# A block of conv, attention and experts: engine order from a list-scheduling pass

## The reference, cut to what matters

```python
mod = silu(c) @ w_ada + b_ada            # sh1, sc1, g1, sh2, sc2, g2, each 1024 wide
hc  = modulate(rmsnorm(ctx), csh1, csc1); k_ctx, v_ctx = context_kv(hc, w_in)
h   = modulate(rmsnorm(x), sh1, sc1)
b, cg, xin, q, k, v, ga, gb = split_in(h @ w_in)
ya  = (b * conv3(cg * xin)) @ w_a
yb  = window_attention(rope(q), rope(k), v, k_ctx, v_ctx, sink) @ w_b   # 8 heads, window 128
x   = x + g1 * ((sigmoid(ga) * ya + sigmoid(gb) * yb) @ w_o)
h   = modulate(rmsnorm(x), sh2, sc2)
x   = x + g2 * hierarchical_moe(h)       # 32 experts, top 2 of the best group
out = rmsnorm(x) * final_g
```

## Time and profile before

| | |
|---|---|
| median of 3 runs | 1257.78 us (1255.66 to 1257.82) |
| profiled execution | 1262.3 us; span of its slowest core, core 1, 1260.6 us |
| PE, DVE, ACT, POOL busy on core 1 | 852.7, 574.9, 394.2, 345.9 us |
| shortest span of a core | 1202.1 us (core 6) |
| DMA | 139.6 MB moved on core 1, mean 111 GB/s |

### The profile page before, as it was taken

The page is one execution under the profiler, slowest core; times in us unless marked ns, Lnnn a source line. Parts: engine busy times, 40 slices in busy tenths (PEclk is TensorE's granted clock), DMA queues, the critical chain, the costliest instruction groups (busy, mean ns, idle before and its releaser), DMA issues. The chain is left out here.

```text
span 1260.6 us, 15879 instructions; the slowest of 8 cores (1202.1 to 1260.6 us)
## 1 busy us (share of the span) xinstructions
PE 852.7 (68%) x6066; PEld 496.3 (39%) x6066; DVE 574.9 (46%) x956; ACT 394.2 (31%) x747; POOL 345.9 (27%) x346
## 2 busy tenths in 40 slices
PE   0035666688698998999999212688688888888500
PEld 0012323343344543444444111466466566666400
DVE  0016333336498133355555257544344344344498
ACT  0022222124344444533333121033233333334332
POOL 2000000022234122202020002356545555565200
PEclk9996878889789899999999755799899999989855
DMA  9952110059750301010206940169999798988473
GB/s 188 198 94 84 51 50 17 1 86 174 123 93 8 61 1 68 1 68 26 76 34 129 175 113 17 56 116 187 200 185 175 147 195 164 190 151 157 129 294 150
DMA packets 41228, 139.61 MB, mean 111 GB/s; under 512 B 14640, under 2 KB 19376, under 8 KB 33600
## 3 DMA queue, kind: packets, MB, share of 16 engines
q0 software_dynamic: 24544, 97.39, 42.3%
q1 hardware_dynamic: 16608, 41.21, 9.6%
HBM read 255.22 MB, written 37.22 MB: 232 GB/s over the span
## 5 line engine op out<-in xcount | busy, mean ns | idle before, releaser
L357 PE MATMUL ps<-sb 128*128 128x512 bf16 (+8 forms) x4976 | 792.6, 317 | 208.9 <-DVE sb L381 136.7
L357 PEld LDWEIGHTS ps<-sb 128*128 128x128 bf16 (+2 forms) x4976 | 428.9, 105 | 551.4 <-issue 182.3
L364 ACT ACTIVATE sb<-ps 128x512 bf16<-128x512 f32 (+4 forms) x593 | 317.3, 584 | 580.2 <-PE ps L357 474.8
L369 DVE TENSOR_TENSOR sb<-ps,sb 128x256 bf16<-128x256 f32 (+4 forms) x262 | 124.6, 482 | 339.7 <-PE ps L357 172.1
L378 DVE SCALAR_TENSOR_TENSOR sb<-sb 128x1024 f32<-128x1024 f32 (+6 forms) x125 | 140.8, 1136 | 12.7 <-DMA sb<-yd 10.0
L1054 POOL DMA_INDIRECT yd<-sb x94 | 99.6, 1059 | 146.0 <-ACT sb L364 132.5
L369 POOL TENSOR_TENSOR sb<-sb 128x1024 bf16<-128x1024 f32 x14 | 32.9, 2346 | 335.3 <-DVE sb L378 298.0
L669 POOL TENSOR_TENSOR sb<-sb 128x512 bf16<-128x512 bf16 x60 | 71.6, 1193 | 156.4 <-ACT sb L364 149.7
L1005 POOL DMA_INDIRECT sb<-hd,sb x94 | 96.7, 1028 | 61.6 <-DVE sb L896 33.6
L369 DVE TENSOR_TENSOR sb<-sb 128x512 bf16<-128x512 f32 (+4 forms) x113 | 86.8, 768 | 35.7 <-issue 31.1
L378 DVE SCALAR_TENSOR_TENSOR sb<-sb,ps 128x512 f32<-128x512 f32 x64 | 43.8, 687 | 129.0 <-PE ps L357 125.5
(11 more groups left out here) (37 smaller groups left out, 144.2 us busy)
## 6 DMA issues: line engine op xcount, KB each, us to landing
sb<-wex POOLq DMA_DIRECT2D x47, 1536.0 KB
sb<-x SPq DMA_DIRECT2D x32, 512.0 KB, 5.1
sb<-wad POOLq DMA_DIRECT2D x12, 1024.0 KB, 16.7
sb<-wsl POOLq DMA_DIRECT2D x8, 1024.0 KB, 44.1
sb<-yd SPq DMA_DIRECT2D x16, 512.0 KB, 5.7
out<-sb SPq DMA_DIRECT2D x16, 512.0 KB, 3.2
hd<-sb SPq DMA_DIRECT2D x16, 256.0 KB, 2.0
sb<-wab POOLq DMA_DIRECT2D x2, 1024.0 KB, 24.4
```

The costliest lines, as they stand in the source:

```text
L357: ins = e.matmul(o, lhsT=l, rhs=r, start=s0, stop=s1)
L364: S.op("act", lambda e: e.activation(out=out, in_=in_, func=func, scale=scale), reads=[in_] + list(extra), writes=w)
L369: S.op(eng, lambda e: e.tensor_tensor(out=out, in0=a, in1=b, op=op), reads=[a, b], writes=[out])
```

## The change

After recording, `Sched.order(300)` replays the recorded operations in a model: each operation has a cost in us (`_cost`, or one given with it), a transfer is issued by its engine and then served by one DMA server for all queues, one after another. At every moment each free engine takes the earliest recorded operation whose inputs are ready, if it lies at most 300 places behind the oldest one not yet done. The order that comes out replaces the recorded one for every engine; dependences stay.

With it the hand-made delays go (`n1_step`, `proj_step`, `att_steps`), the sink load moves to second place and its exponential behind the projections in the recorded order, two of the six early expert loads stay where they were and four wait for the last store of `hd`, and slices 6 and 7 of the second modulation (gate2) are recorded beside the gates of chunk 2, with one buffer of their own in the space of the attention probabilities.

```diff
+    def order(self, window, lat=0.15):
...
+                if ready[e][0] > oldest + window:
+                    continue
+                i = heapq.heappop(ready[e])
...
+                if o["dma"] is not None:
+                    dfree = max(dfree, end + 1.0) + cd
+                    end = dfree + 1.0
...
+        self.ops = [ops[i] for i in out]
...
         sdma(ccs, cc_d, "c_cc")
+        sdma(esb, sink_d.partition_broadcast(128), "c_sink")
...
-        sdma(esb, sink_d.partition_broadcast(128), "c_sink")
         sdma(brtb, brt_d.partition_broadcast(128), "c_brt")
...
-        act(esb, esb, AF.Exp)
         act(scf, ccs, AF.Silu)
...
         def n1_step(t):
             def f():
...
+                n1_sq(t)
+                rs_a(rstd[:, t:t + 1], ss[:, t:t + 1])
+                recip(rstd[:, t:t + 1], rstd[:, t:t + 1])
+                n1_copy(t, n1_apply(t))
...
+        wsb = [wsx[0], wsx[1], view(P0, 4096, BF16)]
+
         def mod2_load(n):
-            gdma(wsx[n % 2], wad_d[4 + n], ("wsx", n % 2))
...
+            i = n % 2 if n < 6 else 2
+            gdma(wsb[i], wad_d[4 + n], ("wsx", i))
...
-        weave(gs_(2), n2_steps(0))
+        weave(gs_(2) + [(2.5, mod2_step(6)), (2.5, mod2_step(7))], n2_steps(0))
...
-        for i in range(4):
+        for i in range(2):
             W(i)
...
-        W(4); W(5)
+        for i in range(2, 6):
+            W(i, [("hd", 15)])
...
+        S.order(WINDOW)
         S.emit()
```

190 lines of the change are left out of this document (117 added, 73 removed).

## The result

The changed kernel takes about 1059 us instead of 1257.8: 0.842 of the time before, with an interval of 0.839 to 0.846 (a fresh series gave 0.842, 0.831 to 0.853). The profiled execution took 1058.06 us, its slowest core is again core 1, and its span fell from 1260.6 to 1056.3 us. (Executions in which one die was slowed are left out of every ratio here.)

A forecast was written before the change was run, and what follows sets the result against it. On core 1, PE's matmul work was taken to bound the gates; most of the rest was waiting. Terms -41 - 51 - 20 - 4 + 4 - 29 + 7 - 17 = -151 took the median from 1257.8 to 1107 us, range 1065 to 1160.

The forecast's parts named there:

- Term 1: Front, up to the first projection: no more wait for the sink load, DVE waits for x tile 5; -41 us.
- Rival 3: Front: loads come in order of issue, as the pass assumes; first projection at 61 us, time 1089 us; chance 0.08.
- Term 2: Chunks 0 to 3 and first queries: PE's waits for normalised tiles go, except one between chunks 0 and 1; -51 us.
- Rival 2: Chunks: the waits stay because the new order only moves each tile's chain; no gain there, 1158 us; chance 0.10.
- term 3: Attention with convolutions: the 16.12 us wait for a weight slice goes and two slices leave the stretch; -20 us.
- term 4: Gates with attention: half of the 9.3 us in which PE is idle goes; -4 us.
- term 6: Second norm: DVE's 31.11 us wait for a store behind six expert loads goes, 0 to 8 us left; -29 us.
- Term 5: Late modulation slices 6 and 7, computed among the output projections before chunk 3's gates, where PE is full; +4 us.
- Term 7: Routing and first expert: four expert loads now start after the gather buffers are cleared and land later; +7 us.
- Term 8: Experts: half of PE's 51.6 us of waits for DVE's copies goes, 9 us given back to loads; -17 us.
- Core 7 keeps its 346 us: Experts on core 7: the stage stays at 346 us, so that core ends at 1093 us and core 1 stays slowest.

The follow-up runs named there:

- no_pass: The changed kernel without its scheduling pass, so the new recorded order goes to the queues as it is; 1323 us at its fastest, 1.055 of the time before.
- sink_back: The changed kernel with the sink load back in 14th place on SP's queue and its exponential recorded first; 0.843 of the time before.
- share_model: The changed kernel with one server for each issuing queue and other transfer rates in the pass's model; 0.848 of the time before.
- filler: The kernel before the change, with 12 useless matmuls ahead of each tile's transposes from tile 4 on; first score at 272.3 instead of 293.1 us, time ratio 0.992.
- half_load: The changed kernel, fetching a third of each expert's weights in 26 loads after the first six; expert stage 333 to 295 us on core 4, 337 to 294 on core 5.

## Why the prediction was wrong in size

Term 1 (right, 4 us too much): the order of events is as worked out. Tile 5 landed at 63.0 us where I took 58.1 from before, and from its square to the first projection went 19 us where I had 20. One sign was wrong: DVE does not stand still for tile 5 alone but a little for each tile, 2.2 us for tile 5. That the edit of the load is the cause is half right: it is enough without the pass (no_pass) and hardly needed with it (sink_back). Rival 3 is not what after does, since its DVE order waits for tile 5; share_model shows that even 29 us here reach nothing without earlier tiles.

Term 2 (15 us short) is the step that failed most. The one break of 9 us was right to 0.3 us; the 120 us of work and break were mis-sized, they took 105.1. The work was priced with rows of before at half or mixed clock: 41 matmuls at 5.57 us in each of the four chunks, which take 3.91 in after (6.6 us in all), and 32 after an idle stretch at 9.51 in chunk 0, which took 8.44. The rest is spread over the groups and the last stretch, from the end of chunk 2 to the scores, 35 us instead of 40. filler shows the sum: 52 us of waits, about 21 of clock, less the 7.9 us of waits that remain, are 65. Rival 2 did not come.

Terms 3, 4 and 6 were 7, 7 and 8 short. In term 3 the idle time went about as forecast (25.5 to 9.0 us, where 18 were to go). What I left out of the sum was the clock, 0.93 instead of 0.84: busy time fell from 103.25 to 92.47, where I had counted 2 us for the two slices, although the term's own bound gave 87 as the end of that scale. In term 4 I let half of the idle time go, and all of it went (9.3 us to none, the clock from 0.98 to 1.00). In term 6 the bound "left 0 to 8 us" should have been read at 0, and DVE's waits for PE fell by 3.6 us too (the earlier trace rows had no row for these). The store in the earlier trace rows is the second of two: the wait ended on the first, issued at 696.1 and landed at 733.74, which changes nothing in the term. No run separates clock and waits in these three stretches as filler does in the chunks.

Term 5 had the sign right and part of its size hidden in term 3. Term 7 is right (5.5 for 7), in its mechanism too: DVE's wait for the last of the four loads ended 44.2 us after the routing began, where 44.9 were said.

Term 8 (12 us short): half of the copy waits going was right in size (51.6 to 22.6 us on line 444, 28.9 with the transposes), what they were was not, so that size was luck. The 9 us given back to loads were not lost on core 1: PE waits 6.6 us for loads in after, 10.6 in before, where more was forecast. "Core 7 keeps its 346 us" came true for that core (343.4), by the loads that half_load shows.

The range failed because it added the half-widths as squares, as if the errors were independent. Four of them lean the same way, with PE's idle time and clock under one new order, and such errors add up as they are: the misses of terms 2, 3, 4 and 6 alone make 37 of the 53 us.

## What to carry to other kernels

In this kernel 52 us of waits on PE cost 21 us more, in the clock of the work behind them. So a stage that is to be freed of waits is better priced with rows at full clock than with its own. A list scheduler is as good as its transfer model: with one server for each of two queues, rates read from the trace, some loads held back and two slices put back, the same pass gave 0.821 instead of 0.842, and with one rate wrong 0.835. Before an order is blamed for a wait, compare the same place on cores of the other die.

## What the hardware showed unexpectedly

Beside a gather by index on POOL, DVE and ACT often go on from PE's work only about 1 us after the gather's end, on the cores of one die of a chip and not of the other: 12 to 35 of 94 copies late by up to 3.7 us in before and after, none in both kernels without such gathers, which still scatter by index. Which die it is differed between series. Why it is one die, and whether it is PE's signal or PE itself that is late, stays open.

While both queues hold transfers, one of SP lands in turn with one of POOL, whatever their sizes. In after (KB, us from issue to landing), a constant of 512 KB issued by POOL at 7.19 us and a load of 6 KB issued by SP at 8.86:

```profile
sb<-c POOLq DMA_DIRECT2D x1, 512.0 KB, 60.1
...
sb<-wc SPq DMA_DIRECT2D x1, 6.0 KB, 58.6
```

They land at 67.3 and 67.5 us, and the next four pairs within 0.2 us of each other too. The Trainium skill's DMA: Bandwidth & Descriptors, section Queues, rings and completion order, has the engines go round the queues packet by packet; the trace agrees in kind, since the two queues' transfers land alternately, and shows that a small load then pays for the large one beside it.
